# Hybrid decoder step on one core: state-space head pairs moved into the attention loop, decode states in groups of four heads, output projection in two halves of the tokens

## The chip, the cores and the metric

The kernel runs on one core of a Trainium2 chip. The time is that of the device, in microseconds (us), median of the runs of one kernel. Five engines work at once and each runs its own list of instructions strictly in order: TensorE (PE, matmuls; PEld is its weight load), VectorE (DVE), ScalarE (ACT), GpSimd (POOL) and SyncE (SP), which here issues every DMA. They meet only in semaphore waits written in the kernel.

## The reference

One layer reads 512 prompt tokens and 8 decode tokens (520 columns in all) through one input projection and feeds two branches: latent attention over 8 heads and a state-space mixer over 16 heads of width 64 with a state of 128. Their gated outputs are concatenated and go through one output projection with a norm and the residual.

```
h = rmsnorm(x);  q_a, c, kr, z_attn, z_ssm, xbc, dt = split(h @ w_in)
attention, 8 heads: softmax(causal(q_lat . ckv + q_rope . k_rope)) @ ckv @ w_uv, times silu(z_attn)
decode rows: the same over 2048 cached rows each, gathered by a page table
state space, prompt (chunks of 128): y = (C B^T * decay * dt) x + C state exp(a_cum);  state' = decay*state + B^T (x dt)
state space, decode: h = exp(da)*h + (x dt) outer B;  y = h . C         (8 sequences x 16 heads x 64 x 128)
(y + d*x) * silu(z_ssm), rmsnorm over two groups of 512 columns
out = x + rmsnorm(concat(attention, ssm) @ w_out)
```

## The kernel before

All activations lie transposed (feature on the partition, token along the row). The program has four parts.

**Projections.** 40 weight items (34 of the input projection, 6 of the query projection) are loaded, split into a high and a low part (`hi` on ACT, `lo` on DVE), and multiplied in three passes (L1220 to L1222). Decode attention over the cached pages is placed between these matmuls by the table `SLOT`.

**State space.** Eight rounds build the chunk states (`xs_t`, `scaled_x`, `state`). Then eight rounds, one for each pair of heads `t`, do this: a row of decays is loaded from DRAM and broadcast to all partitions (`load_acb`, the tile `dec`, L367); POOL masks it (`masked`, L1163); ACT exponentiates it (`decays`, L587, four instructions a head); DVE multiplies it with C B^T (`head`, L986); PE makes 16 + 6 matmuls (L1456, L1459); DVE assembles y (`y_pair`, L993 to L995); POOL gates (L1184); ACT squares; PE sums the squares (L1440). `dec` has six slots, and the load for a head waits until PE has used its slot (`load_acb`: `sp.wait_ge(p_y, ...)`). After it come the value matrices (L1475), the decode rows' values (L1482) and the first keys.

**Attention.** A loop over 8 heads: PE makes the scores of the next head (L1503, L1504), transposes the probabilities of this one (L1514), makes keys (L1494) and outputs (L1522). DVE masks and takes the maximum (L1032, L1033), ACT exponentiates (L637) and copies (L646), POOL divides (L1203). Between them lie the 64 decode updates of `SAMPLE_SSD`, for each sequence and each tile of 128 state rows: ACT scales `hring` (L594), POOL makes `xb` (L1194) and adds it (L1199), DVE takes the dot product (L1007). `hring` holds two sequences, so SP loads and stores states in turn with the loop. Also here: the group norm of the state-space rows (L1058) and their low parts (L1068).

**Output.** 16 weight items (8 tiles of output rows, two halves of the 16 inner tiles); each item serves both halves of the tokens. Two weight slots. After the last matmul: sum of squares, root, reciprocal, then every output tile is scaled and the residual added on DVE (6 tiles, L1117, L1120) and POOL (2 tiles, L1211, L1213), then stored.

The order in each engine is the order of the calls in the program; nothing plans it.

## Time and profile before

| | us |
|---|---|
| median of 3 runs | 655.98 |
| lowest, highest | 654.75, 661.04 |
| the profiled execution | 662.57 |
| its span | 660.7 |
| busy PE, DVE, ACT, POOL | 561.9, 359.3, 262.3, 156.5 |

The profiled execution is 1.0% above the median, and 1.9 us of it lie outside the span. The four parts end at about 323.5 (projections), 442.2 (the first attention scores start), 548.1 (the first output matmul starts), 640.6 (the last one ends) and 660.7 us.

### The profile page before, as it was taken

Reading aid. Unit: us, or ns where it says so; the run is one execution under the profiler, and the core shown is the slowest. Engines: PE = TensorE matmul, PEld = TensorE weight load, DVE = VectorE, ACT = ScalarE, POOL = GpSimd, SP = SyncE. Lnnn points to the kernel's source line nnn. Section 1 sums busy time; section 2 is a strip of 40 time slices with the busy share of each in tenths; the row PEclk is TensorE's granted clock in tenths of the full one; section 3 lists DMA queues with packets and bytes.
Section 4 is the critical chain, followed back from the end, with each engine's and each line's share of the span. In section 5 each row is a group of like instructions: output and inputs, shape, how many; then the busy total and the mean of one; then the engine's idle time right before and its main releaser. Section 6 shows DMA issues by size and latency. Waiting matters only on the chain.

```text
span 660.7 us, 12504 instructions
## 1 busy us (share of the span) xinstructions
PE 561.9 (85%) x4728; PEld 468.8 (71%) x4728; DVE 359.3 (54%) x782; ACT 262.3 (40%) x573; POOL 156.5 (24%) x236
## 2 busy tenths in 40 slices
PE   5999989999999999999863464999886779999990
PEld 5999989998888888888632342465543448999980
DVE  6566977526666664443383563507875672223227
ACT  7233221325555555434323452336675553212210
POOL 3010000000000000000052573108998840112114
PEclk9999989889999999999976576979998899999996
DMA  8141222736888888886154534101232262333203
GB/s 328 64 160 57 73 80 98 249 134 216 263 267 270 260 267 263 267 272 217 62 120 139 116 86 181 64 0 63 85 108 76 84 256 67 96 96 91 70 1 129
DMA packets 46926, 95.75 MB, mean 145 GB/s; under 512 B 6489, under 2 KB 18114, under 8 KB 46354
## 3 DMA queue, kind: packets, MB, share of 16 engines
q1 hardware_dynamic: 46866, 94.94, 44.9%
q8 instruction: 38, 0.62, 0.4%
q14 instruction: 22, 0.18, 0.1%
HBM read 87.29 MB, written 7.73 MB: 144 GB/s over the span
## 4 chain that ended last, share of the span: by engine, by line
PE 64%; DVE 9%; POOL 7%; DMA 6%; issue 5%; SPq 4%; ACT 4%; DVEq 0%; POOLq 0%; ACTq 0%; PEldq 0%
PE pm L1220 16%; PE pm L1221 14%; PE pm L1222 14%; DMA dec<-ac_dram 4%; PE px L1299 4%; POOL xb L1194 3%; PE px L1315 3%; POOL hring L1199 3%; SPq L375 2%; PE pm L1475 2%; PE pm L1522 1%; DVE u L772 1%; PE pm L1494 1%; POOL dec L1163 1%; DMA w_raw<-in_w_out 1%
## 5 line engine op out<-in xcount | busy, mean ns | idle before, releaser
L1220 PE MATMUL pm<-xw_hi,w_lo 128*128 128x260 f32 x544 | 163.8, 301 | 9.2 <-DVE w_lo L819 8.1
L1221 PE MATMUL pm<-xw_lo,w_hi 128*128 128x260 f32 x544 | 155.8, 286 | 0.0
L1222 PE MATMUL pm<-xw_hi,w_hi 128*128 128x260 f32 x544 | 155.6, 286 | 0.0
L1220 PEld LDWEIGHTS pm<-xw_hi,w_lo 128*128 128x128 f32 x544 | 104.6, 192 | 24.4 <-issue 11.9
L428 ACT ACTIVATE w_hi<-w_raw 128x1024 fp32r<-128x1024 f32 (+1 forms) x54 | 55.7, 1032 | 143.8 <-PE pm L1222 143.0
L708 DVE TENSOR_TENSOR w_lo<-w_raw,w_hi 128x1024 fp32r<-128x1024 f32 (+1 forms) x54 | 65.2, 1208 | 80.3 <-ACT w_hi L428 80.3
L1221 PEld LDWEIGHTS pm<-xw_lo,w_hi 128*128 128x128 f32 x544 | 104.7, 192 | 0.2
L1222 PEld LDWEIGHTS pm<-xw_hi,w_hi 128*128 128x128 f32 x544 | 104.6, 192 | 0.0
L1220 PE MATMUL pm<-mix_hi,w_lo 128*128 128x260 f32 x256 | 72.4, 283 | 1.3 <-DVE mix_lo L1038 1.3
L1221 PE MATMUL pm<-mix_lo,w_hi 128*128 128x260 f32 x256 | 72.5, 283 | 0.0
L1222 PE MATMUL pm<-mix_hi,w_hi 128*128 128x260 f32 x256 | 72.4, 283 | 0.0
L1220 PEld LDWEIGHTS pm<-mix_hi,w_lo 128*128 128x128 f32 x256 | 48.2, 188 | 1.4 <-DVE mix_lo L1038 1.4
L1222 PEld LDWEIGHTS pm<-mix_hi,w_hi 128*128 128x128 f32 x256 | 48.3, 189 | 0.0
L1221 PEld LDWEIGHTS pm<-mix_lo,w_hi 128*128 128x128 f32 x256 | 48.2, 188 | 0.0
L1456 PE MATMUL pm<-dec,xdt 128*64 128x128 f32 x128 | 13.2, 371 | 34.5 <-DVE dec L986 34.4
L1157 POOL COPY xlast<-xbc 128x11 f32<-128x11 f32 x12 | 2.3, 194 | 163.8 <-DVE xbc L730 163.8
L1522 PE MATMUL pm<-pt,v 128*128 128x512 f32 (+3 forms) x64 | 25.3, 500 | 16.7 <-ACT pt L646 16.7
L1456 PEld LDWEIGHTS pm<-dec,xdt 128*64 128x64 f32 x128 | 10.4, 191 | 40.4 <-DVE dec L986 40.4
L1171 POOL TENSOR_TENSOR xdte<-xdt,toend 128x512 f32<-128x512 f32 x8 | 10.3, 1297 | 117.5 <-DVE xdt L959 117.5
L1199 POOL TENSOR_TENSOR hring<-hring,xb 128x128 f32<-128x128 f32 x64 | 31.0, 484 | 30.4 <-ACT hring L594 25.1
L587 ACT ACTIVATE dec<-dec,nacum 128x128 f32<-128x128 f32 x64 | 20.4, 389 | 41.8 <-POOL dec L1163 41.8
L1194 POOL TENSOR_SCALAR xb<-bcs,dxs 128x128 f32<-128x128 f32 x64 | 33.3, 520 | 3.5
(250 smaller groups left out, 1096.2 us busy)
## 6 DMA issues: line engine op xcount, KB each, us to landing
page<-in_cache SPq DMA_DIRECT2D x128, 288.0 KB, 3.4
w_raw<-in_w_in SPq DMA_DIRECT2D x34, 512.0 KB, 5.1
w_raw<-in_w_out SPq DMA_DIRECT2D x16, 512.0 KB, 3.6
dec<-ac_dram SPq DMA_DIRECT2D x16, 256.0 KB, 10.5
...
```

The source lines that it names most:

```text
L428: act.activation(w_hi[s][:, 0:n], w_raw[s][:, 0:n], ACT.Copy).then_inc(a_whi, 1)
L587: act.activation(dec[:, h % 6, CH * c:CH * c + CH], dec[:, h % 6, CH * c:CH * c + CH], ACT.Exp, bias=nacum[:, SH * c + h:SH * c + h + 1]). ...
L708: dve.tensor_tensor(w_lo[s][:, 0:n], w_raw[s][:, 0:n], w_hi[s][:, 0:n].bitcast(F), ALU.subtract)\
L1194: pool.tensor_scalar(xb, bcs[:, t // 4, seq, :], dxs[:, 0, t, seq:seq + 1], 0.0, ALU.mult, ALU.add)\
L1199: pool.tensor_tensor(x, x, xb, ALU.add).then_inc(g_h, 1)
L1220: pe.matmul(out, wl, xh, start=start, stop=False)
L1221: pe.matmul(out, wh, xl, start=False, stop=False)
L1222: return pe.matmul(out, wh, xh, start=False, stop=stop)
L1299: last = pe.matmul(px[32 * j:32 * j + 32, n % 2, lo_:lo_ + n_], w, x, start=op == 0, stop=op == 3)
L1315: last = pe.matmul(px[32 * j:32 * j + 32, 3, 0:KVR], ptb[:, n % 2, 32 * j:32 * j + 32], page[:, n % 4, j, 0:KVR], start=True, stop=True)
L1456: pe.matmul(pm[64 * hh:64 * hh + 64, k, CH * c:CH * c + CH], xdt[:, c, HD * h:HD * h + HD], dec[:, h % 6, CH * c:CH * c + CH], start=True, ...
L1522: pe.matmul(pm[:, 3, P * kb:NT], v[:, kb, VH * h:VH * h + VH], pt[:, toff(kb):toff(kb) + NT - P * kb], start=kb == 0, stop=kb == 3).then_i ...
```

## The change

- **Memory.** `hring` now holds all eight decode states (32 KB a partition), on the place of `xdt` and `st`, which are free once the last pair is done. `dec`, the value matrices `v`, `pr`, `pt`, `ea` and the weights have places of their own. So the decay rows of heads 0 to 5 can be loaded as soon as the cached pages are done with, before the projections end, and the value matrices are made between the state rounds.
- **Attention loop.** Two pairs of state-space heads go into each of the first four attention heads. PSUM: the scores rotate over three banks (four before), keys, transposed probabilities and group sums share two banks (`RING`), a pair has two banks of its own (two pairs of two before), so PE waits for DVE after each pair. `ea`, `w_uk` are loaded piece by piece.
- **Group norm.** The squares are added on POOL (`add_square`), one matmul a group remains; the scaling moves from DVE to POOL (`group_scale`).
- **Decode states.** 16 quads (4 tiles each) in place of 64 tiles, after the last pair: six in the last three heads, ten in the first half of the output projection. POOL makes two instructions of 128x512 a quad, ACT and DVE as many as before in all.
- **Output.** 32 items in place of 16: first all output rows for tokens 0 to 259, then for the rest. Each weight tile is loaded and split twice. Four weight slots, hi and lo three items ahead. The first half is finished while PE does the second. Stores of the states lie between the weight loads of the second half.

On PE, the pairs of state-space heads. Before they stand in a block of their own, behind the states (px, pm are PSUM tiles; dec the decays, st the states):

```order
L1425 MATMUL px<-xdte_110,btok 128x512 [waits states_done,x_to_end_done,b_cb_copied]
L1435 MATMUL px<-cm,cvs 32x128 [waits b_cb_copied,conv_sample_silu]
L1456 MATMUL pm<-dec,xdt 64x128 [waits xdt_done,states_done,decay_cb_done]
L1456 MATMUL pm<-dec,xdt 64x128 x7
L1459 MATMUL pm<-xbc,st 128x128 x3
L1456 MATMUL pm<-dec,xdt 64x128 [waits xdt_done,y_done,states_done,decay_cb_done]
```

In the changed kernel they stand within a head, here from the transposes of head 0 on:

```order
L1732 MATMUL pm<-cm,pr 128x128 [waits probs_normed] x2
L1690 MATMUL px<-dec,xdt 64x128 [waits xdt_done,states_done,decay_cb_done]
L1690 MATMUL px<-dec,xdt 64x128 x7
L1693 MATMUL pm<-xbc,st 128x128 x3
L1714 MATMUL pm<-ckv,w_uk 128x512 [waits w_uk_loaded0,ring_read]
...
L1740 MATMUL pm<-pt,v 128x128 [waits ring_read]
L1690 MATMUL px<-dec,xdt 64x128 [waits xdt_done,y_done,states_done,decay_cb_done]
L1690 MATMUL px<-dec,xdt 64x128 x7
L1693 MATMUL pm<-xbc,st 128x128 x3
```

The second pair of a head waits for `y_done` of the first, which DVE gives in the same head.

On ACT, the loop of the changed kernel at head 2 (ea and dec belong to the pairs, pr, pt and kn to the attention, sq are the squares):

```order
L725 ACTIVATE pr,rsum<-px,nmx 128x512
L733 ACTIVATE pt<-pm 128x384
L738 ACTIVATE mix_hi<-u_122 128x520
L705 ACTIVATE ea<-ea 128x384
L688 ACTIVATE dec<-dec,nacum 128x128 x4
L716 ACTIVATE kn<-pm 128x512
L688 ACTIVATE dec<-dec,nacum 128x128 x4
L733 ACTIVATE pt<-pm 128x256
L733 ACTIVATE pt<-pm 128x128
L546 ACTIVATE sq_123<-xbc 128x512
L705 ACTIVATE ea<-ea 128x384
L688 ACTIVATE dec<-dec,nacum 128x128 x8
```

The exponentials of the decays (four instructions a head) now stand between copies that PE waits for.

On SP, the second half of the output projection (w_raw the weight slots, o_ssms the decode states going out); before there were only weight loads here, two slots in turn:

```order
L490 DMA xres_u<-in_xT 128x520
L345 DMA w_raw_92<-in_w_out 128x1024
L422 DMA o_ssms<-hring 128x1024
L345 DMA w_raw_93<-in_w_out 128x1024
L422 DMA o_ssms<-hring 128x1024
...
L345 DMA w_raw_93<-in_w_out 128x1024
L500 DMA o_y<-outp_81 128x260
```

Eight weight loads in turn with eight stores of states, then loads alone, then the stores of y by halves.

The core of the diff. The tables of the order:

```diff
 ITEMS = ([("in", j) for j in range(10)] + [("qb", j) for j in range(6)] + [("in", j) for j in range(10, 34)]
-         + [("out", m, k) for m in range(8) for k in range(2)])
+         + [("out", h, m, k, 1 - k if h == 0 else k) for h in range(2) for m in range(8) for k in range(2)])
...
-SHARE = 6
+SHARE = 5
...
-SAMPLE_SSD = [[0], [1], [2], [3], [4], [5, 6], [7], []]
+RING = [("k", 0), ("k", 1)]
+for _h in range(H):
+    RING += [("t", _h, 0), ("t", _h, 1)] + ([("k", _h + 2)] if _h + 2 < H else []) + [("t", _h, 2), ("t", _h, 3)]
+    RING += [("sum", _h // 2 - 1)] if _h in (3, 5) else []
...
+SLOT_QUADS = {5: {1: 0, 3: 1}, 6: {1: 2, 3: 3}, 7: {1: 4, 3: 5}}
+ITEM_QUADS = {NIN + 6 * (n // 5) + n % 5: 6 + n for n in range(10)}
```

SP, the decay rows that now come before the end of the projections, and the later ones:

```diff
+        sp.wait_ge(s_acd, 16)
+        sp.wait_ge(p_pn, 29)
+        for h in range(4):
+            load_acb(h)
+        sp.wait_ge(p_pn, 30)
+        load_acb(4)
+        load_acb(5)
...
+        for t in range(5):
+            load_acb(2 * t + 6)
+            load_acb(2 * t + 7)
+            load_ea(t + 2)
```

PE, the loop over the heads:

```diff
             probs_t(h, 0)
             probs_t(h, 1)
+            if h < 4:
+                y_pair(2 * h)
             if h + 2 < H:
                 keys(h + 2)
             outs(h, 0)
...
             outs(h, 3)
+            if h < 4:
+                y_pair(2 * h + 1)
+            if h in (3, 5):
+                group_sum(h // 2 - 1)
```

POOL, one quad of decode states:

```diff
+        def state_update(n):
...
+            pool.wait_ge(s_bcs[b % 2], 16 * (b // 2 + 1))
...
+            pool.tensor_tensor(xb, bcs[b % 2][:, g:g + 1, :].to_broadcast(quad),
+                               dxs[:, 0, 4 * g:4 * g + 4, b:b + 1].to_broadcast(quad), ALU.mult).then_inc(g_xb, 1)
...
+            pool.wait_ge(a_h, 4 * n + 4)
+            x = hring[:, b, 4 * g:4 * g + 4, :]
+            pool.tensor_tensor(x, x, xb, ALU.add).then_inc(g_h, 1)
```

DVE, the finish of a half, one output tile after each item from the 22nd on (`done`), and the last half:

```diff
+            if i == NIN + NOUT + 4:
+                inverse(5, r_pre, (0,))
+                dve.wait_ge(s_xr, 32)
+            done = i - NIN - NOUT - 5
+            if 0 <= done < SHARE:
+                finish(0, done)
+                residual(0, done)
+        inverse(5, r_pre, (1,))
+        for m in range(SHARE + 1):
+            if m < SHARE:
+                finish(1, m)
+            if m:
+                residual(1, m - 1)
```

## Rows read from the trace of the kernel before

**Rows 1.** The page, its head.
```profile
span 660.7 us, 12504 instructions
```

**Rows 2.** Windows by stage: us, busy PE, PEld, DVE, ACT, POOL, PEclk, DMA share, GB/s.
```profile
0.00:323.50 323.50, 309.80 (x3315) 280.65 (x3315) 190.59 (x385) 132.90 (x261) 13.20 (x30) 0.98 0.60 194
323.50:350.50 27.00, 17.68 (x75) 10.53 (x75) 18.86 (x34) 10.18 (x21) 14.19 (x11) 0.87 0.53 125
350.50:415.50 65.00, 30.72 (x187) 22.17 (x188) 30.27 (x41) 23.77 (x65) 27.57 (x21) 0.64 0.43 127
415.50:442.20 26.70, 24.48 (x74) 12.21 (x74) 7.25 (x5) 8.99 (x15) 1.62 (x2) 0.88 0.12 40
442.20:548.10 105.90, 84.74 (x302) 49.47 (x302) 72.94 (x270) 64.75 (x186) 80.54 (x159) 0.93 0.31 110
548.10:640.60 92.50, 92.48 (x768) 92.32 (x768) 24.35 (x33) 20.13 (x25) 11.12 (x6) 1.00 0.24 69
640.60:660.70 20.10, 2.04 (x9) 1.44 (x8) 15.08 (x16) 1.56 (x3) 8.22 (x8) 0.69 0.28 106
```

**Rows 3.** Timeline of SP, 305 to 440: start, us, its DMA issues.
```profile
330.67 15.25 SPq L375 DMA_DIRECT2D ea<-ac_dram  x6
...
362.14 30.03 SPq L367 DMA_DIRECT2D dec<-ac_dram  x10
```

**Rows 4.** Waits, whole span: total us, times, longest.
```profile
POOL dec L1163 <- DMA dec<-ac_dram: 31.0, 9, 15.6
```

**Rows 5.** Timeline of PE, one pair of state-space heads.
```profile
392.72 1.09 PE L1456 MATMUL pm<-dec,xdt 128*64 128x128 f32 x16
393.74 0.94 PE L1459 MATMUL pm<-xbc,st 128*128 128x128 f32 x6
```

**Rows 6.** Timeline of PE, where two heads of the attention loop start.
```profile
484.54 0.39 PE L1503 MATMUL px<-kn,q 128*128 128x128 f32 x2
...
495.95 0.39 PE L1503 MATMUL px<-kn,q 128*128 128x128 f32 x2
```

**Rows 7.** Windows, one head of the attention loop.
```profile
486.50:498.00 11.50, 9.87 (x40) 5.88 (x39) 8.84 (x34) 7.84 (x24) 10.44 (x21) 1.00 0.26 92
```

**Rows 8.** Groups by line, whole span: busy us, mean ns of one, idle before.
```profile
L1163 POOL TENSOR_TENSOR dec<-dec,cm 128x512 f32<-128x512 f32 x16 | 21.3, 1341 | 31.0 <-DMA dec<-ac_dram 31.0
L587 ACT ACTIVATE dec<-dec,nacum 128x128 f32<-128x128 f32 x64 | 20.4, 389 | 41.8 <-POOL dec L1163 41.8
L986 DVE TENSOR_TENSOR dec<-dec,cbt 128x512 f32<-128x512 f32 x16 | 12.6, 791 | 32.4 <-ACT dec L587 32.3
L995 DVE TENSOR_TENSOR xbc<-xbc,u 128x384 f32<-128x384 f32 x8 | 7.8, 974 | 0.3
L739 DVE RECIPROCAL sqs<-sqs 128x512 f32<-128x512 f32 x1 | 3.4, 3352 | 4.6 <-ACT sqs L459 4.6
L459 ACT ACT_TABLE_LOAD x1 | 1.3, 1283 | 0.0
```

**Rows 9.** Groups by form, 461 to 495 us.
```profile
L1007 DVE CUSTOM_DVE_ANT_0 prod<-hring,bcs 128x128 f32<-128x128 f32 x24 | 8.0, 332 | 2.9 <-DVE ys L1007 1.6 <-POOL hring L1199 1.3
```

**Rows 10.** Groups by line, 571 to 617 us (output projection).
```profile
L708 DVE TENSOR_TENSOR w_lo<-w_raw,w_hi 128x1024 fp32r<-128x1024 f32 x8 | 9.8, 1226 | 33.1 <-ACT w_hi L428 33.1
L428 ACT ACTIVATE w_hi<-w_raw 128x1024 fp32r<-128x1024 f32 x8 | 8.5, 1060 | 35.7 <-PE pm L1222 35.7
```

**Rows 11.** Windows, 80 us of the projections with page loads.
```profile
200.00:280.00 80.00, 79.60 (x998) 68.23 (x998) 47.07 (x106) 42.03 (x89) 0.58 (x3) 1.00 0.84 265
```

**Rows 12.** DMA issues of the page: count, KB, median us to landing.
```profile
dec<-ac_dram SPq DMA_DIRECT2D x16, 256.0 KB, 10.5
```

**Rows 13.** Tail: timeline of DVE beside POOL and alone.
```profile
650.79 1.22 DVE L1120 TENSOR_TENSOR outp<-outp,xres 128x520 f32<-128x520 f32 x1
...
654.85 0.69 DVE L1120 TENSOR_TENSOR outp<-outp,xres 128x520 f32<-128x520 f32 x1
```

**Rows 14.** Tail: groups by line, 640.5 to 661 us.
```profile
L1211 POOL TENSOR_TENSOR outp<-outp,r_pre 128x260 f32<-128x260 f32 x4 | 4.4, 1090 | 12.5 <-DVE r_pre L739 12.5
```

More of the change, by code:

```diff
@@ new lines, in _ @@
+            if 1 <= s <= 3:
+                exp_ea(2 * s)
+                decays(4 * s + 2)
+            if s + 2 < H:
+                copy_k(s + 2)
+            if 1 <= s <= 3:
+                decays(4 * s + 3)
+            copy_pt(s, 2)
+            copy_pt(s, 3)
+            for b in range(4):
+                for n in quads(s + 1, b):
+                    state_decay(n)
+            if 1 <= s <= 4:
+                gated_square(2 * s - 1)
+            if 1 <= s <= 3:
+                exp_ea(2 * s + 1)
@@ new lines, in dots @@
+        def dots(n):
+            b, g = n // 2, n % 2
+            dve.wait_ge(g_h, n + 1)
+            for t in range(4 * g, 4 * g + 4):
+                if n or t:
+                    dve.wait_ge(v_dot, 8 * b + t)
+                dve.tensor_tensor_reduce(out=prod, in0=hring[:, b, t, :], in1=bcs[b % 2][:, 2 + g, :],
+                                         scale=1.0, scalar=0.0, op0=ALU.mult, op1=ALU.add,
+                                         accum_out=ys[:, t, b:b + 1]).then_inc(v_dot, 1)
@@ L1113, in _ @@
-        inverse(5, r_pre)
-        dve.wait_ge(s_xr, 16)
+        dve.wait_ge(v_os, 1)
+        for s in range(-1, H):
+            h = s + 1
+            for b in range(4):
+                if h < H:
+                    mask_max(h, b)
+                if b == 0 and 2 <= s <= 3:
+                    head(4 * s)
+                    head(4 * s + 1)
+                if b == 1 and 1 <= s <= 4:
+                    y_pair(2 * s - 1)
+                for n in quads(s, b):
+                    if n:
+                        dots(n - 1)
+                if h < H and b:
+                    inverse_sum(h, b - 1)
+            if h < H:
+                inverse_sum(h, 3)
+            if s < 0:
+                continue
+            if s in (4, 6):
+                inverse(s // 2 + 1, (r_pre, sqs)[s // 2 - 2])
+            if s:
+                mix_low(s - 1)
+            if 1 <= s <= 3:
+                head(4 * s + 2)
+                head(4 * s + 3)
+            if s <= 3:
+                y_pair(2 * s)
+            for t in SSM_LOW.get(s, ()):
+                ssm_low(t)
+            gated(s)
+            if s in (5, 6):
+                lo(NIN + s - 5)
@@ L1479, in _, with ring_bank @@
[L1479 to L1495 removed]
+        def ring_bank(use):
+            n = RING_AT[use]
+            if n >= 2:
+                pe.wait_ge(a_ring, n - 1)
+            return pm[:, 1 + n % 2, :]
@@ L1497, in scores, with group_sum, keys @@
+        def group_sum(g):
+            out = ring_bank(("sum", g))
+            pe.wait_ge(g_sqg, 3 * g + 3)
+            pe.matmul(out, cm[:, M_ONE, :], gacc, start=True, stop=True).then_inc(p_ring, 1)
+        def keys(h):
+            out = ring_bank(("k", h))
+            pe.wait_ge(s_ukl[h % 2], 16 * (h // 2 + 1))
+            for r in range(2):
+                last = pe.matmul(out, w_uk[:, h % 2, r, :], ckv[:, r, 0:NT], start=r == 0, stop=r == 1)
+            last.then_inc(p_ring, 1)
         def scores(h):
-            pe.wait_ge(a_k, h + 1)
+            pe.wait_ge(a_ring, RING_AT["k", h] + 1)
@@ L1523, in outs @@
                       start=kb == 0, stop=kb == 3).then_inc(p_o, 1)
-        keys(0)
-        pe.wait_ge(a_rt, 8)
+        xs_t(0)
+        xs_t(1)
+        for n in range(2 * NCH):
+            values_up(n)
+            state(n)
+            if n + 2 < 2 * NCH:
+                xs_t(n + 2)
+        pe.wait_ge(a_cvs, 2)
+        pe.wait_ge(a_cp, 4)
+        pe.transpose(px[0:32, 3, 0:P], cvs[:, 1, 8:12, :], cm[:, M_ID, :]).then_inc(p_bct, 1)
+        pe.wait_ge(v_xdt, 2 * NCH)
+        keys(0)
+        pe.wait_ge(a_v, 7)
+        keys(1)
+        pe.wait_ge(a_bct, 1)
+        for h in range(H):
+            for r in range(2):
+                last = pe.matmul(px[:, 3, 128 + NB * h:128 + NB * h + NB], w_uv[h // 4][:, r, VH * (h % 4):VH * (h % 4) + VH],
+                                 olT[:, r, :, :].rearrange("p g (j k) -> p (g j) k", j=4)[:, :, h],
+                                 start=r == 0, stop=r == 1)
+        last.then_inc(p_os, 1)
+        pe.wait_ge(v_st, 2 * NCH)
+        scores(0)
         pe.wait_ge(v_os, 1)
-        scores(0)
-        keys(1)
+        pe.wait_ge(a_v, 8)
         for h in range(H):
@@ L1570, in _ @@
-        norm_total(5)
+            xl = (mixlo_a, mixlo_s)[k2]
+            for k in range(8):
+                if (i, k) in FIRST_NEEDS:
+                    pe.wait_ge(v_mlo, FIRST_NEEDS[i, k])
+                c = slice(P * k, P * k + P)
+                last = three(pm[:, n % 4, 0:HALF], w_lo[s][:, c], w_hi[s][:, c], xl[:, k, halves[h]],
+                             mix_hi[:, 8 * k2 + k, halves[h]], kk == 0 and k == 0, kk == 1 and k == 7)
+            last.then_inc(p_acc if kk == 1 else p_half, 1)
```

911 lines of the change are left out of this document (487 added, 424 removed).

## The prediction, made before the changed kernel ran

> **What bounds the kernel now.** I read the windows by stage first, because a change of order is worth what its stage can give. Until 323.5 us PE is 96% busy, in the output projection 100% [rows 2]. Between them lie 224.6 us, 27.0 + 65.0 + 26.7 + 105.9, in which PE is busy for 157.6; in the 65 us of the state-space pairs it is busy for 30.7 at a granted clock of 0.64, so mostly at the lower of its two levels, and no other engine passes 31. That stage is a single chain: POOL waits 31.0 us for the decay rows [rows 4], a load lands after 10.5 us [rows 12], and SP issues `ea` for 15.25 us and the last ten decay loads over 30.03 us [rows 3]. The attention loop has another bound: a head starts every 11.4 us (495.95 minus 484.54) [rows 6], POOL is busy for 10.44 of 11.5 us and PE for 9.87 [rows 7]. POOL's load there is mostly the decode updates. The tail is 20.1 us with PE nearly idle [rows 2].
>
> **The sum, against the profiled span of 660.7 [rows 1].**
>
> *Projections*, 323.5: same lists on all engines, one addition, six decay loads near 313 and 318 us after the last pages. 0.
>
> *323.5 to the first scores.* The state rounds stay, 27.0 us [rows 2]. Into them go the value matrices, up to 8 x 0.9 us of PE, which was busy for 17.7 of the 27 us; I count +2.5 for the weights `w_uv`, which are now issued at about 325.5 behind the early decay loads, and +2.5 because PE's third value matrix waits for an ACT copy that stands behind the decode convolution. Then keys, decode values, three decay multiplies: +7.5, near the 26.7 less the values. Sum 39.5: first scores at 363 instead of 442.2. Gain 79. Bounds: 32 (nothing but the 27 and half of the rest) and 53.7 (27.0 + 26.7, nothing hidden).
>
> *Attention loop with the pairs.* Per head without decode work PE needs 9.9 [rows 7]; a pair is 1.8 us at full clock (393.74 + 0.94 - 392.72, less pipeline overlap) [rows 5], two pairs make 13.5. ACT: 7.8 less 2.7 for eight state scalings (start to start), plus 16 decay exponentials (from 5.1 back to back to 16 x 0.389 = 6.2), two `ea`, two squares, 2.2 together: 12.4 to 13.5. DVE: 8.8 less dots (8 x 0.41) and the group scaling 0.9, 4.6; plus 4 x 0.79 for the decays, 2 x 2.5 for y (each of its three instructions at most 0.97): 12.8. POOL: 2.2 for the division, 4 masks, 2 gates, 2 sums of squares at 1.34 each: 12.9 [rows 7 to 9]. So in heads 1 to 3 four engines are equally full, and now hand work round in a circle: DVE's first y comes behind its masks and behind ACT's exponentials of the decays, PE's second pair waits for that y (`y_done`), and the copies of the transposed probabilities stand behind the exponentials too. Writing one head out in order, I find PE's second pair starting at about 15.5 instead of 12.4: 17.8 us a head. Bounds: 14.9 (13.5 by the 10% that a head now lies above its fullest engine, 11.5 against 10.44) and 21 (13.5 with all of the decay exponentials and the y of a pair in series). Head 0 lacks the decays: 14.5. Head 4 has a pair's y left and a reciprocal of 3.35 on DVE and two table loads of 1.28 on ACT [rows 8]: 13.5. Head 5 two quads, two table loads: 13.5. Head 6: DVE has 5.2 of attention, 3.35, 3.4 of dots, 1.9 of low parts and a weight split of 1.2, so 15.5. Head 7 only outputs, behind ACT's copies: 9. With 4.3 for the first scores: 4.3 + 14.5 + 53.4 + 13.5 + 13.5 + 15.5 + 9 = 123.7. Stretches at the lower clock level, as where PE was least busy before: the loop stood at 0.93 [rows 2], and I add 5. Between the last outputs and the first output matmul 1.8. End of the loop: 363 + 123.7 + 5 + 1.8 = 493.5, against 548.1.
>
> A quad costs POOL two instructions of 128x512, 2 x 1.34 = 2.7 [rows 8], an estimate, since before has them only at 128x128. Six quads lie in heads 5 to 7 and are hidden there: POOL has 2.2 + 5.4 + 2.7 of scaling, 10.3 under 13.5.
>
> *Output.* The same 768 matmuls: 92.5 [rows 2]. An item is now 2.9 us. ACT needs 1.06 and DVE 1.23 for each [rows 10], twice as many in all; both fit. In the first eleven items ten quads are added: ACT 1.06 + 1.56 + 0.2 = 2.8; DVE 1.23 + 4 x 0.41 + 0.25 = 3.1; POOL 2.7 and a sum of squares. That is a little over 2.9 and eats into a lead of three items (8.7 us), so it costs nothing yet. If the cover went, each 0.3 would count ten times. I add 1.5 for the residual load, which stands before the third pair of weights. 587.5.
>
> *Tail.* Only half of the tokens: square, total, root 1.6; one reciprocal 1.8 instead of two; POOL has three tiles, six instructions at 1.09 to 1.2 = 7.0 [rows 14]; DVE ten of 260 columns, about 6 (a full tile takes 1.15 beside POOL and 0.61 alone by the starts of its rows) [rows 13]; 3.3 until the last store has landed, as now. 13.7 instead of 20.1. Span 601.
>
> With the 1.9 us outside it 603, times 655.98 / 662.57 for the median: **597 us**. As a sum of differences: -79 before the scores, +24.5 in the loop (130.5 against 105.9), +1.5 in the output, -6.4 in the tail.
>
> **A rule against it.** In the tail a DVE addition of two SBUF operands takes 1.22 while POOL works and 0.69 alone, and POOL's 1.09 for 260 columns is long too [rows 13, 14]. The Trainium skill, "SBUF — State Buffer", section on the two sides of SBUF, says that such a DVE instruction and a GpSimd one exclude each other for their whole length. This trace agrees only in part: in one head POOL's 10.44 and DVE's 8.84 [rows 7] hold about 4 us of DVE instructions of that kind, which together with POOL's own work would not fit into 11.5.
>
> **Rivals.**
> 1. *DVE and POOL take turns* (10%). In the first half of the output, split, dots and quad in series are 1.23 + 1.33 + 2.7 = 5.3 us an item against 2.9 (the dot at 0.332 [rows 9]): ten items, 24 us, less the lead of 8.7, so +15: 612. In heads 1 and 2 it gives 12.9 + 4.3, below my 17.8, so nothing more. This is the time by the rule of the paragraph before.
> 2. *The loop reaches its fullest engine* (13%). Heads 1 to 3 at 14.9, no stretch at the lower clock, first scores at 355: 9 + 5 + 8 less, and half a microsecond less in three later heads: 573. For it: PE at 1.00 and 86% in a head [rows 7]. Against: there only one engine was full.
> 3. *The ring of decays starves the loop* (12%). The slots for heads 6 to 15 come free one pair at a time, and a load takes 10.5 us to land [rows 12]; then mask, exponential and multiply, 3.4, before PE can use it. With 21 to 26 us in heads 1 to 3 and PE at the lower clock level for half of the loop (0.64 to 0.72 as in the old block [rows 2]), 20 to 45 more: 617 to 642. For it: this chain is what bounds the block now. Against: in the new order a slot has a whole head, 14 us, to come back.
> 4. *Slower than before: the output projection becomes DMA-bound* (3%). It moves 30 weight items of 0.52 MB, 4.2 MB of states out, 2.1 MB of residual, 1 MB of broadcasts and 2.1 MB of y, about 25 MB against 6.4 now (69 GB/s over 92.5 us). At the 265 GB/s of the projections [rows 11] that is 94 us, exactly PE's time; at the 127 GB/s at which the old block ran with its small pieces [rows 2] it is 197 us, +104: 700. It decides from about 160 GB/s downward, where 25 MB take the 64 us more that are gained. Against: the pieces are 4 KB a partition, as in the projections, only the stores are new.
> 5. *No change* (2%): there would have to be a wait that takes back 59 us and no more.
>
> The forecast has 60%, from 580 to 615 as its own range. **Range** 572 to 626: it takes in rivals 1 and 2 and the nearer part of 3. A measurement of this kernel tells about 1%; faster by over 1%: 0.95, within 1%: 0.015, slower 0.035.
>
> **What would show each step.** First score matmul at 363 (355 to 377). No wait of POOL for decay loads above 5 us, PE's wait on `y_done` in heads 1 to 3 about 3 us a head. Heads 1 to 3 at 17.8, heads 4 and 5 near 13.5, PE's clock above 0.85 in the loop. First output matmul near 493, item time 2.9 throughout; longer items in the first eleven mean rival 1, in items 18 to 26 rival 4. Tail 13.7. I am wrong if a pair's y costs DVE far more than 2.5 beside POOL, or if the PE clock falls in heads 0 to 3.

## The result, and the profile after

The changed kernel takes 629.66 us, median of 4 runs (628.45 to 630.71); the kernel before took 656.38 beside it. The ratio is 0.958, 95% interval 0.954 to 0.962: faster by 4.2%. The forecast was 597 with a range of 572 to 626. The sign was right, the size was not: 59 us were forecast, 27 came, and the result lies 3.7 us outside the range.

The profiled execution of the kernel before is a slow one (662.57 against the median of 656.38) and that of the changed kernel is the fastest of its four (628.45), so that the stages of the two add up to a difference of 34.2 us where the medians differ by 26.7.

The profiled execution of the changed kernel has a span of 626.5 us. These are its the windows by stage, in the columns of [rows 2]; the stages are the projections, the state rounds up to the first score matmul, the heads up to the first output matmul, the output projection, the tail.

```profile
0.00:321.00 321.00, 307.39 (x3315) 278.27 (x3315) 190.46 (x385) 132.85 (x261) 13.17 (x30) 0.98 0.61 199
321.00:371.00 50.00, 39.35 (x151) 22.22 (x148) 24.01 (x40) 21.33 (x50) 18.14 (x14) 0.86 0.29 84
371.00:503.00 132.00, 100.37 (x479) 62.65 (x478) 91.99 (x205) 76.39 (x203) 76.72 (x76) 0.91 0.30 80
503.00:612.60 109.60, 98.77 (x774) 96.58 (x775) 83.95 (x157) 49.81 (x90) 44.99 (x38) 0.97 0.64 223
612.60:626.50 13.90, 1.39 (x7) 0.57 (x5) 8.97 (x12) 0.86 (x2) 5.06 (x6) 0.73 0.22 77
```

The separate block of 65 us [rows 2] is gone: from the end of the projections to the first output matmul it is 182.0 us instead of 224.6. The output projection, 92.5 us at PE 100% before, is now 109.6 with PE idle for 10.8 of it; the other 6.3 us are longer matmuls, at a granted clock of 0.97 instead of 1.00. The tail fell from 20.1 to 13.9. So 42.6 + 6.2 came from the middle and the tail, 2.5 from the projections, which end earlier in this execution, and 17.1 were given back in a stage in which PE did not wait before.

Against the forecast, by differences: first scores at 371.0 instead of 363 (+8.0), heads with the gap behind them 132.0 instead of 130.5 (+1.5), output 109.6 instead of 94 (+15.6), tail 13.9 instead of 13.7: 25 us in the span. Another 6 us is the factor 0.990 (median over profiled execution of before), by which I scaled the sum. The last 1.2 us are that the profiled execution of the changed kernel lies below its median (628.45 against 629.66), not above it.

**Where the output stage waits.** Waits of the window 503 to 560: total us, times, longest.

```profile
POOL xb L1386 <- DMA bcs<-bc_dram: 17.9, 4, 6.6
ACT w_hi L529 <- DMA w_raw<-in_w_out: 15.0, 7, 4.0
PE pm L1458 <- DVE w_lo L844: 10.0, 6, 2.9
```

PE waits for DVE's low part of the weights, which comes too late by up to 2.9 us. Two kinds of loads are late too: which of these is the cause, a list of waits does not tell. The groups of DVE and POOL in the same stage, 503 to 560, in the columns of [rows 8]:

```profile
L1134 DVE CUSTOM_DVE_ANT_0 prod<-hring,bcs 128x128 f32<-128x128 f32 x40 | 27.7, 692 | 2.2 <-POOL hring L1391 1.2
L844 DVE TENSOR_TENSOR w_lo<-w_raw,w_hi 128x1024 fp32r<-128x1024 f32 x14 | 19.6, 1400 | 4.0 <-ACT w_hi L529 3.9
L1391 POOL TENSOR_TENSOR hring<-hring,xb 128x512 f32<-128x512 f32 x10 | 16.8, 1675 | 7.5 <-ACT hring L696 6.9
L1386 POOL TENSOR_TENSOR xb<-bcs,dxs 128x512 f32<-128x512 f32 x10 | 10.8, 1079 | 18.3 <-DMA bcs<-bc_dram 17.9
```

A dot takes 0.692 us on average; I had counted 0.41, from 0.332 in [rows 9] with its accumulator read. One item shows why. First DVE, then POOL, over the same microseconds (start, duration):

```profile
523.73 1.22 DVE L844 TENSOR_TENSOR w_lo<-w_raw,w_hi 128x1024 fp32r<-128x1024 f32 x1
524.87 1.38 DVE L1134 CUSTOM_DVE_ANT_0 prod<-hring,bcs 128x128 f32<-128x128 f32 x1
...
529.14 0.28 DVE L1134 CUSTOM_DVE_ANT_0 prod<-hring,bcs 128x128 f32<-128x128 f32 x1
```

```profile
522.61 1.05 POOL L1386 TENSOR_TENSOR xb<-bcs,dxs 128x512 f32<-128x512 f32 x1
523.73 2.36 POOL L1391 TENSOR_TENSOR hring<-hring,xb 128x512 f32<-128x512 f32 x1
```

POOL's addition and DVE's split start together at 523.73. The split takes its usual 1.22; the addition takes 2.36, which is the 1.26 of its shortest plus 1.10, about the 1.14 from the start of the split to the start of the next dot. The dot that starts at 524.87 takes 1.38 and ends 0.16 us after POOL's addition; the one at 529.14, with POOL idle, takes 0.28. Both engines' recorded durations hold the time in which the other one has its turn.

An estimate from these rows shows what it costs: 40 dots at 0.28 and 14 splits at 1.22 would be 28.3 us, and 47.3 are recorded, so DVE stands held up for 19 of the 57 us. PE does 116 matmuls of the high part of the activations with `w_lo` (L1458) in them, 14.5 items of 8, which at 2.9 us an item is 42: it loses 15.

### The profile page after: what moved, and what is told of

Same layout as the page of the kernel before. It is cut to its first block, busy times and chain, and to the rows that moved or that the text cites. A ratio compares the mean times of both kernels' runs of the same rounds, so it can differ in the third digit from the quotient of the medians.

```text
span 626.5 us, 12457 instructions
## 1 busy us (share of the span) xinstructions
PE 547.3 (87%) x4716; PEld 460.3 (73%) x4716; DVE 399.4 (64%) x798; ACT 281.2 (45%) x606; POOL 158.1 (25%) x164
## 4 chain that ended last, share of the span: by engine, by line
PE 62%; DVE 18%; issue 6%; ACT 6%; DMA 4%; POOL 3%; SPq 1%; DVEq 0%; POOLq 0%; ACTq 0%
PE pm L1458 15%; PE pm L1460 12%; PE pm L1459 12%; PE px L1541 4%; DVE prod L1134 3%; PE px L1557 3%; DVE w_lo L844 3%; PE pm L1676 2%; DMA w_raw<-in_w_out 2%; DMA w_uv<-in_w_uv 2%; PE pm L1714 1%; PE px L1723 1%; ACT w_hi L529 1%; PE px L1724 1%; PE px L1667 1%
## 5 line engine op out<-in xcount | busy, mean ns | idle before, releaser
L1458 PE MATMUL pm<-xw_hi,w_lo 128*128 128x260 f32 x544 | 163.6, 301 | 9.1 <-DVE w_lo L958 8.1
L1460 PE MATMUL pm<-xw_hi,w_hi 128*128 128x260 f32 x544 | 155.3, 286 | 0.0
L1458 PEld LDWEIGHTS pm<-xw_hi,w_lo 128*128 128x128 f32 x544 | 104.3, 192 | 24.4 <-issue 11.9
L529 ACT ACTIVATE w_hi<-w_raw 128x1024 fp32r<-128x1024 f32 (+1 forms) x70 | 72.2, 1036 | 105.4 <-PE pm L1460 81.7
L844 DVE TENSOR_TENSOR w_lo<-w_raw,w_hi 128x1024 fp32r<-128x1024 f32 (+1 forms) x70 | 88.3, 1265 | 28.1 <-ACT w_hi L529 28.1
L1458 PE MATMUL pm<-mix_hi,w_lo 128*128 128x260 f32 x256 | 75.0, 293 | 16.3 <-DVE w_lo L844 10.0
L1458 PEld LDWEIGHTS pm<-mix_hi,w_lo 128*128 128x128 f32 x256 | 49.6, 194 | 18.6 <-DVE w_lo L844 12.0
L1134 DVE CUSTOM_DVE_ANT_0 prod<-hring,bcs 128x128 f32<-128x128 f32 x64 | 38.4, 599 | 6.9 <-POOL hring L1391 5.1
L1459 PE MATMUL pm<-mixlo_s,w_hi 128*128 128x260 f32 x128 | 36.9, 288 | 0.0
L1459 PE MATMUL pm<-mixlo_a,w_hi 128*128 128x260 f32 x128 | 36.8, 288 | 0.0
L935 DVE SCALAR_TENSOR_TENSOR ckbc<-ckbc,alpha,px 128x256 f32<-128x256 f32 x32 | 15.4, 480 | 25.2 <-PE px L1557 24.6
L1723 PE MATMUL px<-kn,q 128*128 128x128 f32 (+3 forms) x64 | 24.4, 464 | 7.8 <-ACT pr L725 7.7
L601 ACT ACTIVATE alpha<-nmh 128x1 f32<-128x1 f32 x32 | 9.4, 295 | 44.4 <-DVE nmh L924 44.3
L725 ACT ACTIVATE pr<-px,nmx 128x128 f32<-128x128 f32 (+3 forms) x32 | 16.8, 524 | 27.8 <-DVE nmx L1164 27.8
```

What stands on the lines that cost most here:

```text
L529: act.activation(w_hi[s][:, 0:n], w_raw[s][:, 0:n], ACT.Copy).then_inc(a_whi, 1)
L725: act.activation(pr[:, h % 2, i0:i0 + n], px[:, n_ % 3, 0:n], ACT.Exp, bias=nmx[:, k:k + 1], accum_out=rsum[:, k:k + 1])\
L844: dve.tensor_tensor(w_lo[s][:, 0:n], w_raw[s][:, 0:n], w_hi[s][:, 0:n].bitcast(F), ALU.subtract)\
L935: dve.scalar_tensor_tensor(ckbc[:, g, :], ckbc[:, g, :], alpha[:, n:n + 1], px[:, 3, 0:KVR], ALU.mult, ALU.add)\
L1134: dve.tensor_tensor_reduce(out=prod, in0=hring[:, b, t, :], in1=bcs[b % 2][:, 2 + g, :], scale=1.0, scalar=0.0, op0=ALU.mult, op1=ALU.add, ...
L1458: pe.matmul(out, wl, xh, start=start, stop=False)
```

## The experiments

Ten kernels, all timed against the kernel before. "Output" is the time from the first to the last start of the first matmul of an output item's three passes (`mix_hi` with `w_lo`, L1458 in the changed kernel), in the profiled execution; the kernel before has 92.0 by the same measure.

| kernel | ratio to before, 95% interval | median us | first scores | output from | output |
|---|---|---|---|---|---|
| changed kernel | 0.958 [0.954, 0.962] | 629.7 | 371.0 | 503.0 | 109.3 |
| no dots | 0.936 [0.931, 0.941] | 615.6 | 371.6 | 501.5 | 97.4 |
| no POOL updates | 0.932 [0.927, 0.937] | 614.6 | 373.9 | 504.5 | 97.5 |
| C rows in PSUM | 0.942 [0.937, 0.946] | 619.2 | 372.0 | 503.6 | 98.8 |
| w_uv early | 0.944 [0.939, 0.949] | 620.4 | 361.5 | 498.0 | 111.2 |
| residual late | 0.972 [0.966, 0.977] | 637.1 | 373.3 | 504.1 | 113.7 |
| pairs in a block | 1.095 [1.086, 1.104] | 717.7 | 485.3 | 589.8 | 111.0 |
| POOL in pieces | 0.975 [0.968, 0.981] | 639.7 | 372.2 | 508.4 | 116.5 |
| PSUM and w_uv | 0.930 [0.923, 0.938] | 611.6 | 366.0 | 499.9 | 96.7 |
| block, running ahead | 0.995 [0.991, 0.999] | 656.0 | 422.1 | 526.8 | 108.6 |
| reordered as well | 0.921 [0.915, 0.927] | 608.6 | 363.9 | 497.7 | 96.4 |

Beside four of the kernels (residual late, pairs in a block, POOL in pieces, PSUM and w_uv) the runs of the kernel before lay between 650.9 and 663.9, so their ratios are the less certain ones. The runs of residual late (634.0 to 639.3), POOL in pieces (635.9 to 642.9) and PSUM and w_uv (604.5 to 613.4) do not overlap with those of the changed kernel (628.5 to 630.7).

**1. No dots (e1_no_dots).** The decode part of y is left out.

```diff
-                dve.tensor_tensor_reduce(out=prod, in0=hring[:, b, t, :], in1=bcs[b % 2][:, 2 + g, :],
-                                         scale=1.0, scalar=0.0, op0=ALU.mult, op1=ALU.add,
-                                         accum_out=ys[:, t, b:b + 1]).then_inc(v_dot, 1)
+            dve.nop().then_inc(v_dot, 4)
```

> The changed kernel without the 64 dot products of the decode heads on DVE (DVE only counts the semaphore up; the decode part of y is left out). Theory 1, DVE and POOL take turns: the dots, 1.0 to 1.4 us each beside a POOL instruction of a quad, are what fills DVE past PE's 2.9 us an item; without them DVE has one split an item, at most 2.1 us. The output goes from 109.5 to about 95, the gap before it from 5.5 to 3, head 6 loses 2: 629.7 - 19 = 611. Theory 2, late weight loads (ACT waits 15.0 us for w_raw between 503 and 561): the loads stay, so 625 or more. Theory 3, DVE is simply too full by its own work and POOL has no part in it: 611 too; the next kernel tells it from theory 1.

Measured: 615.6, output 97.4. The 12 us of the output go. ACT still waits 8.0 us for weight loads in the first 57 us of the output, and PE for a split only 0.6. That speaks against the loads as the cause; between a full DVE and turns it does not decide.

**2. No POOL updates (e2_no_updates).** The two POOL instructions of each quad are left out, and with them the update of the states.

```diff
-            pool.tensor_tensor(xb, bcs[b % 2][:, g:g + 1, :].to_broadcast(quad),
-                               dxs[:, 0, 4 * g:4 * g + 4, b:b + 1].to_broadcast(quad), ALU.mult).then_inc(g_xb, 1)
...
-            pool.tensor_tensor(x, x, xb, ALU.add).then_inc(g_h, 1)
+            pool.nop().then_inc(g_h, 1)
```

> The changed kernel without POOL's two instructions of every quad (the state update is left out; DVE's dots, ACT's scalings and all loads and stores stay). Theory 1: with POOL out of the way every dot takes 0.29 us as when it is alone and the split 1.2, the output falls to about 95 and the total to 609. Theory 2: 625 or more. Theory 3: DVE keeps its own work, the dots keep a mean near 0.6 us, and the total stays above 625.

Measured: 614.6, output 97.5. DVE has the same instructions as in the changed kernel, and they have shrunk (first 57 us of the output):

```profile
L844 DVE TENSOR_TENSOR w_lo<-w_raw,w_hi 128x1024 fp32r<-128x1024 f32 x19 | 23.4, 1242 | 9.1 <-ACT w_hi L529 9.1
L529 ACT ACTIVATE w_hi<-w_raw 128x1024 fp32r<-128x1024 f32 x19 | 20.0, 1054 | 14.7 <-DMA w_raw<-in_w_out 14.2 <-PE pm L1456 0.5
L1134 DVE CUSTOM_DVE_ANT_0 prod<-hring,bcs 128x128 f32<-128x128 f32 x44 | 14.2, 322 | 1.1
```

A dot takes 0.322 instead of 0.692, a split 1.24 instead of 1.40, although nothing was taken from DVE's list. ACT still waits 14.2 us for weight loads, nearly the 15.0 of the changed kernel, and the output does not mind: theory 2 falls. Theory 3 falls too, since DVE keeps its whole work and PE no longer waits. The exclusion is shown, and its price in the output is about 12 us. The total moved by 15 of the 20 us expected. In the profiled execution, 3.5 us above this kernel's median, the first scores came 2.9 us later and heads 1 to 3 took 2.3 us longer than in the changed kernel, although nothing was taken out there; why is not shown.

**3. C rows in PSUM (e3_dots_from_psum).** Nothing is left out. ACT copies the two C rows of a sequence to a free PSUM bank, and the dot has one SBUF operand instead of two.

```diff
+            act.activation(c_in_psum(b), bcs[b % 2][:, 2:4, :].rearrange("p k n -> p (k n)"), ACT.Copy).then_inc(a_cc, 1)
...
-                dve.tensor_tensor_reduce(out=prod, in0=hring[:, b, t, :], in1=bcs[b % 2][:, 2 + g, :],
+                dve.tensor_tensor_reduce(out=prod, in0=hring[:, b, t, :], in1=c_in_psum(b)[:, P * g:P * g + P],
```

> The changed kernel with one operand of the dots (the C rows) copied to PSUM by ACT, one activation of 128x256 for each sequence, so that a dot reads SBUF for one operand only; nothing is left out. Theory 1 in its narrow form, what collides is the second SBUF operand: dots of 0.3 us beside POOL's instructions of the quads, splits still 1.9 to 2.1, DVE at about 3.3 an item instead of 6; the output falls from 109.5 to about 98 and the total to 618. If the length of a dot has nothing to do with where its operand lies (theories 2 and 3, or an exclusion of any DVE instruction): 630, or 2 more for ACT's added copies.

Measured: 619.2, output 98.8, as expected. The same groups in the first 57 us of the output, with POOL's quads in place:

```profile
L861 DVE TENSOR_TENSOR w_lo<-w_raw,w_hi 128x1024 fp32r<-128x1024 f32 x19 | 29.0, 1534 | 5.7 <-ACT w_hi L535 5.7
L1409 POOL TENSOR_TENSOR hring<-hring,xb 128x512 f32<-128x512 f32 x10 | 16.4, 1639 | 9.1 <-ACT hring L702 8.5
L1152 DVE CUSTOM_DVE_ANT_0 prod<-hring,px 128x128 f32<-128x128 f32 x44 | 12.5, 285 | 3.5 <-POOL hring L1409 2.4
L1404 POOL TENSOR_TENSOR xb<-bcs,dxs 128x512 f32<-128x512 f32 x10 | 11.8, 1185 | 2.7 <-DMA bcs<-bc_dram 2.2
```

The dot is at 0.285 beside POOL, while the split, which still has two SBUF operands, is at 1.53. The timeline shows both in one POOL instruction (DVE, then POOL):

```profile
528.26 1.92 DVE L861 TENSOR_TENSOR w_lo<-w_raw,w_hi 128x1024 fp32r<-128x1024 f32 x1
530.10 0.28 DVE L1152 CUSTOM_DVE_ANT_0 prod<-hring,px 128x128 f32<-128x128 f32 x1
530.42 0.29 DVE L1152 CUSTOM_DVE_ANT_0 prod<-hring,px 128x128 f32<-128x128 f32 x1
```

```profile
529.05 1.74 POOL L1445 TENSOR_TENSOR sqs<-sqs,sq 128x260 f32<-128x260 f32 x1
```

Both dots run through while POOL is in an instruction of its own. So not every DVE instruction takes turns with POOL: the dot does with both operands in SBUF, and does not with one of them in PSUM. The Trainium skill, "SBUF — State Buffer", section on the two sides of SBUF, says that the pair of ports is an exclusive lock for the whole instruction, and that DVE competes for it with an instruction that has two SBUF inputs, or with one in a mode that takes both ports for a single input, which it lists for copies. For the dots of this stage the traces agree: 0.28 against 1.38 us. The number of operands alone is not the whole rule here either. In head 7 of the changed kernel a DVE copy of 8 columns, with one SBUF operand, takes 1.22 us beside POOL and 0.16 without it (rows 490.98 and 502.73 in the part on the prediction); no run tried it apart. One more effect came with the PSUM copy: POOL's wait for the B and C rows fell from 17.9 to 2.2 us (0.5 in experiment 1), because their buffer is given back behind the last dot. Most of that late load was a consequence of late dots.

**4. w_uv early (e4_early_uv).**

```diff
-        for h in range(4):
+        for h in range(2):
             load_acb(h)
-        sp.wait_ge(p_pn, 30)
-        load_acb(4)
-        load_acb(5)
         sp.wait_ge(p_pv, 2)
+        sp.dma_start(w_uv[0], a["w_uv"][0]).then_inc(s_kv[0], 16)
         sp.dma_start(stS, a["conv_state"]).then_inc(s_sts, 16)
-        for k in range(2):
-            sp.dma_start(w_uv[k], a["w_uv"][k]).then_inc(s_kv[k], 16)
+        sp.dma_start(w_uv[1], a["w_uv"][1]).then_inc(s_kv[1], 16)
+        for h in range(2, 6):
+            load_acb(h)
```

> The changed kernel with the weights w_uv and the conv state issued behind two of the early decay loads instead of six; the other four follow them. Theory: PE's 6.7 us wait for w_uv at 332.8 comes from the 1.5 MB of small decay pieces in front of it; w_uv lands about 4 us sooner, first score matmul at 367 instead of 371, total 625.7. Rival: the chain from the conv state over DVE's decode convolution (ACT waits 14.5 us for it) or SP's later issues of dxs set that point: first scores at 371 or later, total 629.7 to 632.

Measured: first scores at 361.5, total 620.4: the theory holds and was too small. PE's first value matrix, in the changed kernel and in this one (start, duration, wait before it):

```profile
332.82 3.78 PE L1676 MATMUL pm<-w_uv,ckv 128*128 128x512 f32 x4 [6.71 <-DMA w_uv<-in_w_uv]
...
344.98 2.92 PE L1676 MATMUL pm<-w_uv,ckv 128*128 128x512 f32 x4 [2.81 <-ACT v L710]
```

```profile
326.16 1.98 PE L1675 MATMUL pm<-w_uv,ckv 128*128 128x512 f32 x4
...
335.49 3.65 PE L1675 MATMUL pm<-w_uv,ckv 128*128 128x512 f32 x4 [3.03 <-ACT v L709]
```

The wait goes completely, and the matmul is 1.98 instead of 3.78 us, since the granted clock of this stage is 0.96 instead of 0.86: 9.5 us for moving four loads. The heads then take 136.5 instead of 132.0 us, at 0.87 instead of 0.91; but this profiled execution took 625.3, 4.9 us above the kernel's median, and its granted clock over the whole span is 0.944, where the three fastest have 0.955 to 0.958. So that the heads lose what the state rounds win is seen in one execution, and is not shown for the others. The third value matrix still waits 3.0 us for the ACT copy behind the decode convolution, as forecast (+2.5).

**5. Residual late (e5_late_xres).** The 1.82 MB load moved behind the eighteenth weight item.

```diff
-        sp.dma_start(xres_g, a["xT"][:, 0:7]).then_inc(s_xr, 16)
         for i in range(NIN + 4, NIN + 18):
             load_item(i)
...
         sp.wait_ge(v_mlo, 16)
+        sp.dma_start(xres_g, a["xT"][:, 0:7]).then_inc(s_xr, 16)
```

> The changed kernel with the 1.82 MB of the residual loaded after the eighteenth weight item instead of between the fourth and the fifth. By the theory of turns the weight loads are late because DVE gives their slots back late, so this does little: output 109.5 to about 107, total 627. Rival, late loads: ACT's waits for w_raw in 503 to 561 (15.0 us) come from the residual in front of them; then the hole at 520 to 530 (3.0 us of PE) and more of the 15 go, output about 101, total 621.

Measured: 637.1, slower than the changed kernel; neither number came. Windows of 10 us, of this kernel:

```profile
520.00:530.00 10.00, 6.46 (x52) 6.04 (x50) 5.30 (x14) 5.65 (x13) 6.55 (x6) 1.00 0.87 294
...
570.00:580.00 10.00, 7.56 (x62) 7.35 (x62) 5.00 (x8) 4.53 (x7) 0.00 (x0) 1.00 1.02 417
```

The hole at 520 to 530 is there without the residual (PE 6.46, in the changed kernel 6.98), so it was not its cause. A new one opens at 570 to 580, where the residual now meets the state stores and the weight loads and the DMA engines are full at 417 GB/s. Where the changed kernel puts it, the load costs less.

**6. Pairs in a block, twice.** The matmuls, masks, exponentials and y of the pairs ahead of the heads, all the rest as changed. In the first kernel (e6_pairs_first) DVE took its multiplies for pair t+3 ahead of the y of pair t; the second (e9_pairs_first_ahead) differs by this on DVE, and by ACT's `ea` standing ahead of its exponentials:

```diff
         for t in range(8):
-            if t < 5:
-                head(2 * t + 6)
-                head(2 * t + 7)
             y_pair(t)
+            if 1 <= t <= 5:
+                head(2 * t + 4)
+                head(2 * t + 5)
```

> The changed kernel with the eight pairs (matmuls, masks, exponentials, y) in a block ahead of the attention heads, as before the change; the gates and squares, the early loads, the quads and both output halves stay as changed. Theory: the weaving is what hides the pairs; in a block they cost at least their fullest engine, POOL's ten masks and DVE's y and multiplies, and 4 to 6 us for each returning slot of the decay ring, 45 to 60 us, while the heads fall from 132 to about 105 less the heads' better fill: total 655 (645 to 670). Rival: most of the gain is from the early decay loads, the tail and the moved decode work, the weaving brings little: 635 or less.

> As the kernel with the pairs in a block (e6), but with DVE's y of a pair ahead of its multiplies for the pair three later, and ACT's ea ahead of its exponentials, so that the block runs two to three pairs ahead of its loads. In e6 PE waited 12 us a pair for a y that stood behind a whole return trip of the decay ring (block 371.9 to 485.3, 113.4 us). Theory: the serial trip was e6's own fault; the block now costs 55 to 65 us as in the kernel before, and the total comes to 665 (655 to 675), still more than before the change has. Rival: the ring's return trip limits it in any order, 690 or more.

The first took 717.7, far above both expectations, and the cause is in the order: the y of a pair stood behind a load that could start only once the pair's slot was free, so each pair waited for the whole return trip. Its largest wait (total, times, longest):

```profile
POOL dec L1321 <- DMA dec<-ac_dram: 92.2, 10, 18.9
```

The second ran 656.0, at the lower end of the 655 to 675 expected, and it is the experiment that counts (its profiled execution is the fastest of its ten, 4.5 us below their median). Block and heads in its windows:

```profile
371.50:422.10 50.60, 25.02 (x177) 21.13 (x178) 20.73 (x32) 14.82 (x46) 13.36 (x10) 0.58 0.38 76
422.10:526.80 104.70, 83.32 (x302) 48.23 (x301) 72.35 (x172) 64.05 (x157) 63.05 (x66) 0.89 0.18 65
```

50.6 + 104.7 = 155.3 us, where the woven heads take 132.0. The difference of the ratios, 0.995 less 0.958, is 24 us: nearly the whole gain of the change, as far as this order of the block goes. The two orders differ by 62 us, and a third was not tried. Without the weaving, all its other parts (early decay loads, later quads, token halves) come to 0.5% together: of what the middle and the tail gain, the output, 109.2 us here, takes back 16.7. The block itself was 65.0 before [rows 2], 14 us more; how much of that is due to the early loads was not tried apart. In the new block POOL still waits 37.2 us for decay loads.

**7. POOL in pieces (e7_pieces).**

```diff
-            pool.tensor_tensor(xb, bcs[b % 2][:, g:g + 1, :].to_broadcast(quad),
-                               dxs[:, 0, 4 * g:4 * g + 4, b:b + 1].to_broadcast(quad), ALU.mult).then_inc(g_xb, 1)
+            for t in range(4 * g, 4 * g + 4):
+                pool.tensor_scalar(xb[:, t % 4, :], bcs[b % 2][:, g, :], dxs[:, 0, t, b:b + 1], 0.0, ALU.mult, ALU.add)\
+                    .then_inc(g_xb, 1)
...
+                pool.tensor_tensor(x, x, xb[:, t % 4, :], ALU.add).then_inc(g_h, 1)
```

> The changed kernel with each quad of POOL as eight instructions of 128x128 (0.40 and 0.46 us each in the kernel before) instead of two of 128x512 (1.1 to 1.5 us), dots released piece by piece. If DVE and POOL take turns by whole instructions, a dot waits 0.4 to 0.5 us at most, its mean falls from 0.60 to about 0.5, but POOL's own time grows from 2.7 to 3.4 a quad and the sum of the two engines does not fall: 628 to 636. Rival: the size of POOL's instruction is what costs, short ones slip between the dots: 620 or less.

Measured: 639.7, output 116.5: above the 628 to 636 of the theory and far from the rival's 620. The first 57 us of the output:

```profile
L1386 POOL TENSOR_SCALAR xb<-bcs,dxs 128x128 f32<-128x128 f32 x39 | 26.4, 677 | 4.0 <-POOL hring L1391 1.0
L1391 POOL TENSOR_TENSOR hring<-hring,xb 128x128 f32<-128x128 f32 x39 | 22.3, 572 | 3.2
L1134 DVE CUSTOM_DVE_ANT_0 prod<-hring,bcs 128x128 f32<-128x128 f32 x39 | 13.5, 346 | 22.4 <-POOL hring L1391 21.6
```

The dots are short again, 0.346 where I expected about 0.5, and it helps nothing: now POOL's pieces are long, 0.68 and 0.57 us instead of 0.40 and 0.46, 1.25 for a pair of them, and DVE waits 21.6 us for their results. Small pieces move the waiting from one engine to the other and add to it.

**8. The two gains together (e8_psum_and_uv), and a better order (e10_reordered).** The second adds to the first:

```diff
-            if n == 2:
+            if n == 6:
                 sample_conv()
...
+            if s in (5, 6):
+                gated(s)
             if s:
                 mix_low(s - 1)
...
         mix_low(H - 1)
+        dots(4)
```

(The two activations behind `sample_conv` move with it on ACT, and `dots(4)` stands no longer in head 7.)

> Nothing left out: the C rows in PSUM (e3) and w_uv ahead of four decay loads (e4) together, and the B and C rows of a sequence loaded again once ACT has copied the C rows, not after the last dot. The two gains lie in different stages and should add: ratio 0.958 - 0.017 - 0.015 = 0.927, 610 us. Rival: the earlier start is eaten in the loop, which grew from 132.0 to 136.5 us in e4: 614.

> Nothing left out. On top of the C rows in PSUM and the early w_uv (e8, 611.6): the decode convolution on DVE and its two activations stand in the seventh round instead of the third; in heads 5 and 6 DVE takes the attention product u ahead of the low parts (PE waited 6.95 us for it in e8); the dots of the fifth quad stand behind the last low parts before the output. Theory: PE's 3.0 us wait for the third value matrix and the 6 us around it go (-3 to -5), the wait for u falls to 2 (-4), the one before the output from 4.3 to 3 (-1): 602. Rival: each wait is taken over by the next one in the same round or head (rounds stay at 3.0 us from the state chain, head 6 waits for its scores by 5.96): 609.

Measured: 611.6 and 608.6, with the ratios of the table; nothing is left out in either. e8 comes out at its sum (0.930 against 0.927), its output at 96.7. e10 is nearer to its rival. The wait at the third value matrix (3.03 us in e8) turned up behind the eighth, before the last state matmul, and the one for u (6.95) became a shorter one for ACT:

```profile
354.21 1.70 PE L1691 MATMUL px<-xdte,btok 128*128 128x512 f32 x2 [2.83 <-POOL xdte L1362]
...
486.64 1.12 PE L1764 MATMUL pm<-pt,v 128*128 128x512 f32 x2 [4.04 <-ACT pt L744]
```

The wait for the last low parts before the output, which was to fall from 4.3 to 3, rose to 6.75. So each wait was mostly taken over by the next one. The intervals of the two ratios overlap, so this last step is not shown to be a gain. Both beat the changed kernel.

## Why the prediction came out too low

**Failed: the output term, "that is a little over 2.9 and eats into a lead of three items (8.7 us), so it costs nothing yet".** I took DVE and POOL as independent and added up 3.1 and 2.7 us an item. They take turns: 5.3 us in series, which is my rival 1, to which I gave 10%. Its sign came too: the items of the first 57 us take 3.9 us on average instead of 2.9. It said +15 in the output; the output came out 15.6 over the forecast, and experiments 1 to 3 take 10 to 12 us of that away with the collision, so that the close agreement with rival 1 is partly luck. The rest, 97.4 to 98.8 instead of 92.0, is in part at two places for which the forecast had no term, here by the windows of experiment 1 (97.4). Behind the wait before the stage the granted clock is 0.66 for 5 us, in which PE does 29 matmuls, and 44 in the 5 us behind them: 1.7 us by their count. And PE waits 1.3 us for the low part of the decode rows, which came after the last quad. The other 2.4 us stay open.

**Why I set the rule aside.** I argued that 10.44 us of POOL and 4 us of two-operand DVE work do not fit into a head of 11.5 [rows 7]. A recorded duration contains the time in which an instruction is held up by the other engine, 2.36 instead of 1.26 in the row above, so the sum of two busy times counts the shared stretch twice. The head of [rows 7] has both signs (DVE twice, then POOL):

```profile
486.93 0.87 DVE L1038 TENSOR_TENSOR mix_lo<-u,mix_hi 128x520 fp32r<-128x520 f32 x1
487.73 0.28 DVE L1007 CUSTOM_DVE_ANT_0 prod<-hring,bcs 128x128 f32<-128x128 f32 x1
```

```profile
487.35 0.82 POOL L1194 TENSOR_SCALAR xb<-bcs,dxs 128x128 f32<-128x128 f32 x1
```

POOL's `xb` takes 0.82 beside `mix_lo`; the shortest of its kind is 0.37. But double counting is not all of the answer. With each state instruction at its shortest (0.37 and 0.45), POOL's 21 instructions still come to 9.1 us, and with DVE's 4 to 13.1, more than 11.5: the dot at 487.73 takes its 0.28 within the `xb`. So with pieces of 128x128 the two engines do overlap in part, by recorded times, and my error was to conclude from "not everything in turn" that the long instructions of the output stage do not collide at all. The right reading was in [rows 13]: the same DVE addition at 1.22 and at 0.69.

**Failed in size: first scores at 363.** They came at 371.0, and relative to the end of the projections (321.0) the stage took 50.0 instead of 39.5. I had put +2.5 on w_uv behind the early decay loads; it cost 9.5, as experiment 4 shows, 6.7 of waiting and the rest beside a lower clock. That is 7.0 of the 10.5; the other 3.5 are in the stage without that wait too (40.5 in experiment 4 against my 39.5 less 2.5). I had counted the issue on SP and not the traffic: each of the six decay loads of 256 KB takes 11.3 us to land (median), and w_uv 10.8 behind all six of them but 4.6 behind two (experiment 4). The term for the ACT copy was right (2.8 measured).

**Held in the sum, by luck in its parts: the heads.** The starts of heads 0 to 6, each with the first scores of the next head (start, duration):

```profile
375.39 0.38 PE L1723 MATMUL px<-kn,q 128*128 128x128 f32 x2
389.54 0.39 PE L1723 MATMUL px<-kn,q 128*128 128x128 f32 x2
406.20 0.63 PE L1723 MATMUL px<-kn,q 128*128 128x128 f32 x2
424.28 0.39 PE L1723 MATMUL px<-kn,q 128*128 128x128 f32 x2
445.77 0.38 PE L1723 MATMUL px<-kn,q 128*128 128x128 f32 x2
456.49 0.39 PE L1723 MATMUL px<-kn,q 128*128 128x128 f32 x2
467.84 0.38 PE L1723 MATMUL px<-kn,q 128*128 128x128 f32 x2
```

Head 0 takes 14.2 (forecast 14.5), heads 1 to 3 together 56.2 (53.4), heads 4 and 5 22.1 (27), head 6 17.2 (15.5), head 7 12.5 (9), the gap before the output 5.5 (1.8). The 5 us that I had added for stretches at the lower clock come on top of the forecasts; the measured times contain theirs. The errors cancel, which is luck. Heads 1 to 3 are not three times 17.8 but 16.7, 18.1 and 21.5, the last above my bound of 21: there two multiplies of DVE take 3.33 us beside POOL's masks, where one alone takes 0.69, and the second pair's matmuls 1.98 instead of 1.09 at the lower clock. PE's waits for y are shorter than the 3 us a head that I gave: five, 7.3 in all.

```profile
493.08 2.05 PE L1740 MATMUL pm<-pt,v 128*128 128x512 f32 x2 [7.11 <-DVE u L1179]
502.96 0.56 PE L1458 MATMUL pm<-mix_hi,w_lo 128*128 128x260 f32 x1 [5.51 <-DVE mixlo_s L1188]
```

The first of these two waits is not the quads': without their dots or their updates it is still 6.5 us (experiments 1 and 2). Ahead of u DVE has its low parts and a copy, beside POOL's scaling of the group norm, which the change moved there (DVE in head 7, then the same instructions with POOL idle):

```profile
487.64 3.42 DVE L1188 SCALAR_TENSOR_TENSOR mixlo_s<-xbc,cols,mix_hi 128x512 fp32r<-128x512 f32 x2
490.98 1.22 DVE L1177 COPY u<-z 128x8 f32<-128x8 f32 x1
...
501.41 1.41 DVE L1188 SCALAR_TENSOR_TENSOR mixlo_s<-xbc,cols,mix_hi 128x512 fp32r<-128x512 f32 x2
502.73 0.16 DVE L1177 COPY u<-z 128x8 f32<-128x8 f32 x1
```

That is 3.1 of the 7.1 us; the scaling back on DVE was not tried. The second wait, for the last low parts, does fall, to 2.5 and 1.7 in experiments 1 and 2.

**Rivals 3 and 4 did not occur.** POOL waits for decays twice, 4.8 and 2.5 us (the mark was 5), both in head 1, whose 16.7 us are below the forecast. The output was not bound by DMA: in the window 560 to 580 its engines are full at 366 GB/s and PE is at 97%.

```profile
560.00:580.00 20.00, 19.32 (x158) 19.02 (x158) 13.29 (x30) 9.25 (x13) 0.00 (x0) 1.00 1.00 366
```

**Held: the tail**, 13.9 against 13.7. **Failed: the scaling to the median.** One profiled execution 1% over its median says nothing of where the next one lies.
